# Float32 products replaced by products of parts in the last pooling group, and four steps moved around them

## The chip, the cores and the metric

The kernel runs on one core of one Trainium2 chip, in float32 throughout: inputs, outputs and sums. The metric is the time of one execution on the device in microseconds, the median of several runs. The core's engines are TensorE (matmuls; PE in the profile, and PEld for its weight loads), VectorE (DVE), ScalarE (ACT), GpSimd (POOL) and SyncE (SP), which here only issues transfers.

## What is computed

Two decoder layers on 256 tokens of 2048 features: the first mixes tokens by causal pooling over windows of 2, 4, 8 and 16 tokens, the second by latent attention. Each layer has a SwiGLU feed-forward of width 5632. The change is all in the first layer, from the pooling to the start of its feed-forward:

```python
POOL_WINDOWS = (2, 4, 8, 16)
def multiscale_pool_mixer(h, pool_w, pool_scale):
    cs = jnp.cumsum(hf, axis=1)
    for g, w in enumerate(POOL_WINDOWS):
        sl = slice(g * POOL_GROUP, (g + 1) * POOL_GROUP)      # 512 features
        c_prev = jnp.pad(cs[..., sl], ((0, 0), (w, 0), (0, 0)))[:, :S]
        count = jnp.minimum(t + 1, w)
        diff = (cs[..., sl] - c_prev) / count - hf[..., sl]
        outs.append(jnp.einsum('bsc,cd->bsd', diff, pool_w[g]))   # 512 x 512
    return jnp.concatenate(outs, axis=-1) * pool_scale
...
x = x + multiscale_pool_mixer(rms_norm(x, pool_norm[l]), pool_w[l], pool_scale[l])
x = x + swiglu(rms_norm(x, ffn_norm[l]), w_gate[l], w_up[l], w_down[l])
```

## The kernel before, in words

**Parts.** A float32 matmul is slow on TensorE, so nearly all products are made of parts. ScalarE rounds a number to the type float32r (the high part), VectorE subtracts (the low part), and TensorE adds high x high, high x low and low x high. For weights this is `split`: a chunk of 128 x 1024 lands in one of eight slots of `raw`, ScalarE writes `w_hi` (L850), VectorE writes `w_lo` (L1238), both with four slots, and signals `lo_ready`. For activations it is `gained`: ScalarE multiplies x by the norm's gain into the left half of `xg` (L862), VectorE writes the low part into the right half (L1248). `product3` (L435, L436) then takes one loaded tile of weights against 512 columns (both halves of `xg`), and its low part against 256.

**Pooling.** The pooling is linear over tokens and the product linear over features, so the kernel first multiplies and then mixes. `pool_product(g, half)` (L505) is a plain float32 matmul: `x_pool` (x times gain, made by ScalarE's `pool_gain`) is the loaded tile of 128 x 128, a chunk of pooling weights is the moving one with 512 columns. A group has four feature tiles and two halves of the tokens, so eight matmuls, four for each `half`. `product_hi` on ScalarE (L887) and `product_lo` on VectorE (L1294) scale the result by the token's norm factor `tok_rstd` and leave the parts in `z`. `mix(g)` multiplies `z` by a band matrix over tokens: four outputs of five matmuls each (L527 to L533), of which L530 takes the low part of the band's first 16 columns. `pool_out` (L1300, VectorE) adds an output to x and signals `evacuated`.

**Norm sums.** The feed-forward's norm needs the sum of squares of the new x over all 2048 features. ScalarE squares each of the 16 tiles (`group_squares`, L898) into four buffers, the halves of `cross` and `sums`; GpSimd adds them into `square_sum` (L1737). Its add of tile 10 waits for `lo_ready` to be 4. `sum_over_partitions` (L487) is a TensorE matmul with ones, in the middle of the feed-forward's third pair of chunks. ScalarE's `root_of` (L856) and VectorE's `rstd_of` (L1242) follow, in order ahead of the first `ffn_tile`: `cross` (L928), `sums` (L1318, L1322), and then `split` of chunk up0 + 7.

**Order.** Every engine runs its own list in program order and waits on semaphores. TensorE's list is: products of groups 0 to 2, with `token_squares` (L513) amid the last; mix(0); first half of group 3; mix(1); second half; mix(2); chunk up0 of the feed-forward; mix(3); chunks up0 + 1, + 2, + 3 (`first_tiles`: two tiles at once); then tiles of two chunks each. A chunk is eight times `product3`. VectorE goes group by group: four `pool_out`, four `gained`, `split` of chunk up0 + g, `product_lo(g + 2)` for g < 2. ScalarE does the same with four squares behind each `split`. After group 3 both split chunks up0 + 4 to up0 + 6. Chunks 6 and 7 of `raw` are the pooling weights of group 3.

Of the kernel before, what the change touches and what calls it, by code (L numbers as in the profile page):

```python
# [38 lines left out]
F32 = mybir.dt.float32  # L39
F32R = mybir.dt.float32r  # L40
I32 = mybir.dt.int32
ALU = mybir.AluOpType
ACT = mybir.ActivationFunctionType

P = 128
# [79 lines left out]
def chunk_elems(n):  # L125

    for ph in ("down0", "down1", "down2", "down3"):
        if CHUNK[ph] <= n < CHUNK[ph] + 2 * (LAST_DT if ph == "down3" else DT):
            return DTILES * P
    if CHUNK["heads"] <= n < CHUNK["wo"] and (n - CHUNK["heads"]) % 4 == 0:  # L130
        return TILES * P // 2
    return TILES * P


def made(n):
# [9 lines left out]
def trunk(nc, xT, positions, consts, bands, gains, pool_first, pool_w, w_kv_a, w_k_pe, w_q_a, w_kv_k, w_kv_v, w_q_nope, w_q_pe,  # L145
          w_o, w_gate, w_up, w_down, w_last, final_gain, out):
    with ExitStack() as ctx:
# [124 lines left out]
        squares_ready = sem("squares_ready")  # L272
        quarter_ready = sem("quarter_ready")
        pool_gained = sem("pool_gained")
        square_made = sem("square_made")
        ones_ready = sem("ones_ready")
        init_ready = sem("init_ready")
# [153 lines left out]
        def _(pe):  # L431
# [60 lines left out]
            for _ in range(WARM_UP):  # L492
                pe.matmul(ps[:, SCORES, 0:P], ones[:, :], ones[:, :], start=True, stop=True)  # L493

            def pool_product(g, half):

                c = 2 * g + half
                for j in range(2):
                    kt = 2 * half + j
                    pe.wait_ge(w_part[c] if c < 2 and j == 0 else landed[c], 16)  # L500
                    pe.wait_ge(pool_gained, GT * g + kt + 1)
                    for s in range(2):
                        if kt == 0 and g == 3:
                            pe.wait_ge(z_ready, 2 * (g - 2) + s + 1)
                        mm = pe.matmul(ps[:, product_bank(g, s), :], x_pool[:, GT * g + kt, s * P:(s + 1) * P],  # L505
                                       raw[:, c, j * GT * P:(j + 1) * GT * P], start=(kt == 0), stop=(kt == GT - 1))
                mm.then_inc(chunks_used, 1)
# [9 lines left out]
            def mix(g):  # L517

                pe.wait_ge(z_ready, 2 * g + 2)
                for j in range(GT):  # L520
                    t = GT * g + j
                    if t >= 4 and t not in (12, 13):
                        pe.wait_ge(evacuated, t - 3)
                    bank = mix_bank(t)
                    first_hi, first_lo = (z[:, g % 2, 0, part, j * P:(j + 1) * P] for part in range(2))
                    second_hi, second_lo = (z[:, g % 2, 1, part, j * P:(j + 1) * P] for part in range(2))
                    pe.matmul(ps[:, bank, 0:SEQ], first_hi, band[:, g, B_FIRST:B_FIRST + SEQ], start=True, stop=False)  # L527
                    pe.matmul(ps[:, bank, 0:SPILL], first_lo, band[:, g, B_FIRST:B_FIRST + SPILL], start=False,
                              stop=False)
                    pe.matmul(ps[:, bank, 0:PAD], first_hi, band[:, g, B_LOW:B_LOW + PAD], start=False, stop=False)  # L530
                    pe.matmul(ps[:, bank, P:SEQ], second_hi, band[:, g, B_SECOND:B_SECOND + P], start=False,
                              stop=False)
                    pe.matmul(ps[:, bank, P:SEQ], second_lo, band[:, g, B_SECOND:B_SECOND + P], start=False,  # L533
                              stop=True).then_inc(mixed, 1)
# [16 lines left out]
            def ffn(layer, half, xg_before, stats):  # L551
                p = 2 * layer + half
                n0, t0 = CHUNK[UPS[p]], TILE[UPS[p]]
                peel = 0
                if half == 0:
                    peel = 1
                    if layer == 0:
                        first_tiles(n0, t0, xg_before, (0,))
                        mix(GROUPS - 1)
                        first_tiles(n0, t0, xg_before, (1, 2, 3))  # L560
                    else:
                        first_tiles(n0, t0, xg_before)
                    long_tile(n0 + 4, t0 + 2, xg, TILES,
                              each=lambda kt: sum_over_partitions(stats) if kt == TILES else None)
                    long_tile(n0 + 6, t0 + 3, xg, TILES)
                with pe.Fori(0, FH // 2 - peel) as i:
                    for f in range(4):
                        long_tile(n0 + BODY * peel + 2 * f, t0 + 4 * peel + f, xg, TILES, i, 4)
                n0, t0 = CHUNK[DOWNS[p]], TILE[DOWNS[p]]
                if p == 3:  # L570
                    return

                long_tile(n0, t0, act, DTILES, each=lambda kt: pe.wait_ge(act_ready, p * FH + kt + 1))
                for d in range(1, 4):
                    long_tile(n0 + 2 * d, t0 + d, act, DTILES)
                with pe.Fori(0, DT // 4 - 1) as i:
                    for d in range(4):
                        long_tile(n0 + BODY + 2 * d, t0 + 4 + d, act, DTILES, i, 4)
# [259 lines left out]
        def _(sc):  # L838
# [51 lines left out]
            def group_gained(g):  # L890
                for t in range(GT * g, GT * g + GT):
                    gained(t, TILE["pool"] + t + 1, G_FFN0, xg)

            def group_squares(g):
                for t in range(GT * g, GT * g + GT):
                    if t >= 4:
                        sc.wait_ge(squares_added, t - 3)
                    nc.scalar.activation(square_of(t), x[:, t, :], ACT.Square).then_inc(square_made, 1)  # L898

            sc.wait_ge(gain_landed, 16)  # L900
            pool_gain(0)
# [3 lines left out]
            quarter_square(2)  # L905
            pool_gain(2)
            quarter_square(3)
            pool_gain(3)
            sc.wait_ge(stats_summed, 1)
            nc.scalar.activation(tok_root[:, :, :], ps[:, 0:2, 0:1], ACT.Sqrt, bias=eps[:, :],  # L910
                                 scale=1.0 / D_MODEL).then_inc(root_ready, 1)
            sc.wait_ge(rstd_ready, 1)
            product_hi(0)
            product_hi(1)
            for g in range(GROUPS):
                group_gained(g)
                split(CHUNK["up0"] + g)
                group_squares(g)
                if g < 2:
                    product_hi(g + 2)  # L920

            def ffn_tile(p, f, splits, i=None):

# [13 lines left out]
            def ffn(layer, half, stats):  # L937
                p = 2 * layer + half
                n0 = CHUNK[UPS[p]]
                for w in range(3):  # L940
                    split(n0 + w + SPLIT_SLOTS)
                if stats is not None:
                    root_of(stats, D_MODEL)

                def tile(f, i=None):

                    n = n0 + 4 * f + 3 + SPLIT_SLOTS
                    ffn_tile(p, f, (lambda: split(n, i), lambda: split(n + 1, i),
                                    lambda: (split(n + 2, i), split(n + 3, i))), i)

                with sc.Fori(0, FH // 2 - 1) as i:
                    tile(0, i)
                    tile(1, i)
                tile(FH - 2)

                nothing = lambda: None
                ffn_tile(p, FH - 1, (nothing, nothing, lambda: split(n0 + 4 * FH - 1 + SPLIT_SLOTS)))

                n1, t1 = CHUNK[DOWNS[p]], TILE[DOWNS[p]]
                if p == 3:  # L960
                    return

                def down(d, i=None):
                    split(n1 + 2 * d + SPLIT_SLOTS, i)
                    if half == 1 and layer == 0:
                        gained(d, t1 + d + 1, G_ATTN, xg, i, 4)
                    split(n1 + 2 * d + 1 + SPLIT_SLOTS, i)

                with sc.Fori(0, DT // 4 - 1) as i:
                    for d in range(4):  # L970
                        down(d, i)
                for d in range(DT - 4, DT):
                    down(d)
# [229 lines left out]
        def _(ve):  # L1203
# [71 lines left out]
            for q in range(4):  # L1275
                ve.wait_ge(squares_ready, q + 1)
                a, b, c = x_square[:, 4 * q:4 * q + 2, :], x_square[:, 4 * q + 2:4 * q + 4, :], x_square[:, 4 * q, :]
                step(nc.vector.tensor_tensor(a, a, b, ALU.add))
                ins = nc.vector.tensor_tensor(c, c, x_square[:, 4 * q + 1, :], ALU.add)
                if q >= 1:  # L1280
                    step(ins)
                    ins = nc.vector.tensor_tensor(c, c, x_square[:, 4 * q - 4, :], ALU.add)
                ins.then_inc(quarter_ready, 1)
                ve.wait_ge(quarter_ready, q + 1)
            ve.wait_ge(gain_landed, 16)
            ve.wait_ge(root_ready, 1)
            nc.vector.reciprocal(tok_rstd[:, :, :], tok_root[:, :, :]).then_inc(rstd_ready, 1)
            ve.wait_ge(rstd_ready, 1)
# [13 lines left out]

            product_lo(0)
            product_lo(1)
            for g in range(GROUPS):
                for t in range(GT * g, GT * g + GT):
                    pool_out(t)
# [555 lines left out]
```

## Time and profile before

| | |
|---|---|
| median of 3 runs | 1771.49 us (1771.15 to 1771.55) |
| the profiled execution | 1770.85 us, of it the span of the trace 1769.1 us |
| granted TensorE clock | 0.999 |
| TensorE busy | 1761.5 us |
| VectorE / ScalarE / GpSimd busy | 1130.7 / 914.3 / 113.1 us |
| bytes moved | 328.79 MB, 186 GB/s on average |

A row of the timeline has the start in us from the span's start, the time it took, the engine, the line, the operation, what it writes and reads, and how many like it are merged. In brackets stands how long the engine was idle ahead of it and what released it. The ends of matmuls are modelled, so TensorE's pace is read from one start to the next, best from its weight loads.

### The profile page before, as it was taken

The page shows a single profiled execution, that of the slowest core. Times are in us where ns is not written, and L with a number is a line of the kernel's source. Part 1 is how long each engine was busy: PE and PEld are TensorE (multiplying, and loading weights), DVE is VectorE, ACT ScalarE, POOL GpSimd, SP SyncE. Part 2 cuts the span into 40 slices and gives each one's busy share as a digit, 9 for nine tenths or more (in the row PEclk, how much of TensorE's full clock was granted, in tenths as well). Part 3 has the DMA queues.
Part 4 walks back from the last instruction along what each step waited for, and adds up shares of the span by engine and source line. Part 5 has one row for each costly group of instructions (what it writes and reads, how often), then busy time and mean ns, then how long its engine had stood idle before and what let it go on. Part 6 is the DMA issues. An engine that isn't in the chain of part 4 may idle for free.

```text
span 1769.1 us, 29325 instructions
## 1 busy us (share of the span) xinstructions
PE 1761.5 (100%) x10438; PEld 1564.0 (88%) x10438; DVE 1130.7 (64%) x1460; ACT 914.3 (52%) x1176; POOL 113.1 (6%) x132
## 2 busy tenths in 40 slices
PE   9999999999999999999999999999999999999998
PEld 6888888888888888889999888888888888888887
DVE  5766666556666666678997776666655566666554
ACT  6666664334444453456775466666533344445433
POOL 2100000000000001124111420000000000000000
PEclk9999999999999999999999999999999999999999
DMA  7555556545555566545445555555665455556642
GB/s 282 195 188 190 189 197 229 191 155 177 190 190 190 190 223 196 175 152 160 148 137 179 190 184 191 189 188 188 230 200 166 162 190 190 190 190 222 227 146 72
DMA packets 86017, 328.79 MB, mean 186 GB/s; under 512 B 9680, under 2 KB 11088, under 8 KB 85840
## 3 DMA queue, kind: packets, MB, share of 16 engines
q1 hardware_dynamic: 85680, 327.03, 55.5%
q10 hardware_dynamic: 288, 1.11, 0.2%
q8 instruction: 30, 0.49, 0.1%
q14 instruction: 19, 0.16, 0.0%
HBM read 326.01 MB, written 2.10 MB: 185 GB/s over the span
## 4 chain that ended last, share of the span: by engine, by line
PE 100%; DVE 0%; issue 0%; DVEq 0%; ACT 0%; POOL 0%; POOLq 0%
PE ps L435 58%; PE ps L436 31%; PE ps L505 2%; PE ps L443 1%; PE ps L445 1%; PE ps L444 1%; PE ps L799 1%; PE ps L798 1%; PE ps L797 1%; PE ps L633 0%; PE ps L632 0%; PE ps L631 0%; PE ps L685 0%; PE ps L493 0%; PE ps L705 0%; PE ps L706 0%
## 5 line engine op out<-in xcount | busy, mean ns | idle before, releaser
L1238 DVE TENSOR_TENSOR w_lo<-raw,w_hi 128x1024 fp32r<-128x1024 f32 (+2 forms) x564 | 736.0, 1308 | 419.1 <-ACT w_hi L850 416.9
L435 PE MATMUL ps<-xg,w_hi 128*128 128x512 f32 x2880 | 999.7, 390 | 0.0
L850 ACT ACTIVATE w_hi<-raw 128x1024 fp32r<-128x1024 f32 (+2 forms) x565 | 630.9, 1120 | 548.9 <-PE ps L436 533.2
L436 PE MATMUL ps<-xg,w_lo 128*128 128x256 f32 x2880 | 812.1, 282 | 0.0
L435 PEld LDWEIGHTS ps<-xg,w_hi 128*128 128x128 f32 x2880 | 540.5, 188 | 113.5 <-DVE w_lo L1238 0.3
L436 PEld LDWEIGHTS ps<-xg,w_lo 128*128 128x128 f32 x2880 | 544.3, 189 | 0.1
L435 PE MATMUL ps<-act,w_hi 128*128 128x512 f32 x1320 | 458.0, 390 | 0.0
L436 PE MATMUL ps<-act,w_lo 128*128 128x256 f32 x1320 | 372.2, 282 | 0.0
L435 PEld LDWEIGHTS ps<-act,w_hi 128*128 128x128 f32 x1320 | 247.7, 188 | 51.9
L436 PEld LDWEIGHTS ps<-act,w_lo 128*128 128x128 f32 x1320 | 249.5, 189 | 0.0
L1318 DVE TENSOR_TENSOR sums<-ps,cross 128x512 f32<-128x512 f32 x88 | 60.8, 691 | 93.1 <-ACT cross L928 93.1
L928 ACT ACTIVATE cross<-ps 128x512 f32<-128x512 f32 x88 | 52.5, 597 | 117.4 <-PE ps L436 117.0
L435 PE MATMUL ps<-heads,w_hi 128*128 128x512 f32 x256 | 89.1, 391 | 0.0
L1691 POOL TENSOR_TENSOR square<-x 128x256 f32 (+1 forms) x32 | 33.2, 1038 | 762.6 <-DVE x L1339 762.6
L436 PE MATMUL ps<-heads,w_lo 128*128 128x256 f32 x256 | 72.2, 282 | 0.0
L1338 DVE TENSOR_TENSOR x<-ps,x 128x256 f32 (+1 forms) x76 | 32.1, 422 | 54.6 <-PE ps L436 54.6
L1322 DVE TENSOR_TENSOR sums<-sums,rstd 128x512 f32<-128x512 f32 x88 | 60.9, 692 | 3.0
L931 ACT ACTIVATE gate_act<-sums 128x256 f32<-128x256 f32 x88 | 36.8, 419 | 47.3 <-DVE sums L1322 47.1
L862 ACT ACTIVATE xg<-x,gain 128x256 fp32r<-128x256 f32 (+1 forms) x48 | 23.5, 508 | 66.9 <-DVE x L1339 62.1
L435 PEld LDWEIGHTS ps<-heads,w_hi 128*128 128x128 f32 x256 | 48.0, 188 | 9.9
L436 PEld LDWEIGHTS ps<-heads,w_lo 128*128 128x128 f32 x256 | 48.4, 189 | 0.0
L443 PE MATMUL ps<-latent,w_hi 128*128 128x256 f32 x160 | 44.9, 281 | 0.0
(200 smaller groups left out, 1240.2 us busy)
## 6 DMA issues: line engine op xcount, KB each, us to landing
raw<-w_gate SPq DMA_DIRECT2D x176, 512.0 KB, 3.2
raw<-w_up SPq DMA_DIRECT2D x176, 512.0 KB, 3.2
raw<-w_down SPq DMA_DIRECT2D x120, 704.0 KB, 4.2
raw<-w_o SPq DMA_DIRECT2D x32, 512.0 KB, 3.2
raw<-w_last SPq DMA_DIRECT2D x11, 512.0 KB, 3.2
raw<-w_q_a SPq DMA_DIRECT2D x8, 512.0 KB, 3.2
raw<-w_kv_a SPq DMA_DIRECT2D x8, 512.0 KB, 3.3
raw<-w_q_nope SPq DMA_DIRECT2D x8, 512.0 KB, 3.2
```

What stands on the lines that cost most here:

```text
L435: pe.matmul(ps[:, bank, :], w_hi[:, s, j * P:(j + 1) * P], moving, start=start, stop=False)
L436: return pe.matmul(ps[:, bank, 0:SEQ], w_lo[:, s, j * P:(j + 1) * P], moving[:, 0:SEQ], start=False, stop=stop)
L443: pe.matmul(dst, w_hi[:, s, j * P:(j + 1) * P], moving[:, 0:SEQ], start=start, stop=False)
L505: mm = pe.matmul(ps[:, product_bank(g, s), :], x_pool[:, GT * g + kt, s * P:(s + 1) * P], raw[:, c, j * GT * P:(j + 1) * GT * P], start=(k ...
L850: nc.scalar.activation(dst, src, ACT.Copy).then_inc(hi_ready, 1)
L928: nc.scalar.activation(cross[:, :, :], ps[:, bank:bank + 2, SEQ:], ACT.Copy).then_inc(cross_ready, 1)
L931: nc.scalar.activation(gate_act[:, :], sums[:, 0, :], ACT.Silu).then_inc(gate_ready, 1)
L1238: nc.vector.tensor_tensor(lo, src, hi.bitcast(F32), ALU.subtract).then_inc(lo_ready, 1)
L1318: nc.vector.tensor_tensor(sums[:, :, :], ps[:, bank:bank + 2, 0:SEQ], cross[:, :, :], ALU.add).then_inc(evacuated, 2)
L1322: nc.vector.tensor_tensor(sums[:, :, :], sums[:, :, :], r, ALU.mult).then_inc(sums_ready, 1)
L1338: step(nc.vector.tensor_tensor(xd, ps[:, b, 0:SEQ], xd, ALU.add))
L1691: step(nc.gpsimd.tensor_tensor(square[:, :], src, src, ALU.mult))
```

## The change

Four things are done. Group 3 of the pooling is multiplied in parts: ScalarE writes the high part of x times gain for its four tiles into `xg` and the high part of chunks 6 and 7 into `w_hi`, VectorE writes the low parts, and `split_product` takes three matmuls of 512 columns in place of one float32 matmul. For group 0 (a window of 2, whose factors 1 and 1/2 have no low part) L530 is left out. ScalarE's squares of group 3 are no longer made in one piece: the splits of up0 + 4, + 5 and + 6 stand between them. And `sum_over_partitions` stands four `product3` later in its chunk.

```diff
+def band_is_exact(g):
+    return all(w & (w - 1) == 0 for w in range(1, WINDOWS[g] + 1))
...
+            def split_product(half):
+                c = 2 * (GROUPS - 1) + half
+                w = c % SPLIT_SLOTS
+                pe.wait_ge(pool_w_lo, half + 1)
+                for j in range(2):
+                    kt = 2 * half + j
+                    pe.wait_ge(pool_x_lo, kt + 1)
+                    wh, wl = (part[:, w, j * GT * P:(j + 1) * GT * P] for part in (w_hi, w_lo))
+                    for s in range(2):
+                        if kt == 0:
+                            pe.wait_ge(z_ready, 2 * (GROUPS - 3) + s + 1)
...
+                        pe.matmul(dst, hi, wh, start=(kt == 0), stop=False)
+                        pe.matmul(dst, hi, wl, start=False, stop=False)
+                        mm = pe.matmul(dst, lo, wh, start=False, stop=(kt == GT - 1))
+                mm.then_inc(chunks_used, 1)
...
-                    pe.matmul(ps[:, bank, 0:PAD], first_hi, band[:, g, B_LOW:B_LOW + PAD], start=False, stop=False)
+                    if not band_is_exact(g):
+                        pe.matmul(ps[:, bank, 0:PAD], first_hi, band[:, g, B_LOW:B_LOW + PAD], start=False, stop=False)
...
-                              each=lambda kt: sum_over_partitions(stats) if kt == TILES else None)
+                              each=lambda kt: sum_over_partitions(stats) if kt == TILES + 4 else None)
...
+            def pool_x_split():
+                sc.wait_ge(x_landed[GROUPS - 1], 16)
+                for t in range(DT - GT, DT):
+                    nc.scalar.activation(xg[:, t, 0:SEQ], x[:, t, :], ACT.Identity,
+                                         scale=gain[:, G_POOL + t, :]).then_inc(pool_x_hi, 1)
+
+            def pool_w_split(half):
+                c = 2 * (GROUPS - 1) + half
+                sc.wait_ge(landed[c], 16)
+                nc.scalar.activation(w_hi[:, c % SPLIT_SLOTS, 0:TILES * P], raw[:, c, 0:TILES * P],
+                                     ACT.Copy).then_inc(pool_w_hi, 1)
...
             quarter_square(3)
-            pool_gain(3)
+            pool_x_split()
+            pool_w_split(0)
             sc.wait_ge(stats_summed, 1)
...
             product_hi(1)
+            pool_w_split(1)
...
                 group_gained(g)
+                if g >= 2:
+                    sc.wait_ge(chunks_used, 2 * (GROUPS - 1) + g - 1)
                 split(CHUNK["up0"] + g)
-                group_squares(g)
+                if g < GROUPS - 1:
+                    group_squares(g)
...
-                for w in range(3):
-                    split(n0 + w + SPLIT_SLOTS)
+                if p > 0:
+                    for w in range(3):
+                        split(n0 + w + SPLIT_SLOTS)
...
             ve.wait_ge(gain_landed, 16)
+            for t in range(DT - GT, DT):
+                ve.wait_ge(pool_x_hi, t - DT + GT + 1)
+                nc.vector.scalar_tensor_tensor(
+                    xg[:, t, SEQ:], x[:, t, :], gain[:, G_POOL + t, :], xg[:, t, 0:SEQ].bitcast(F32), ALU.mult,
+                    ALU.subtract).then_inc(pool_x_lo, 1)
+            pool_w_split(0)
             ve.wait_ge(root_ready, 1)
...
             product_lo(1)
+            pool_w_split(1)
```

ScalarE's last squares and the splits of up0 + 3 to up0 + 6, from group 3's `gained` to the root of the norm. Before:

```order
L862 ACTIVATE xg<-x,gain 128x256 x4
L850 ACTIVATE w_hi<-raw 128x1024
L898 ACTIVATE cross<-x 128x256 x2
L898 ACTIVATE sums<-x 128x256 x2
L850 ACTIVATE w_hi<-raw 128x1024 x3
L856 ACTIVATE root<-ps,eps 128x256
```

And with the change (L892, L880, L927 and L886 are the same four lines of code):

```order
L892 ACTIVATE xg<-x,gain 128x256 x4
L880 ACTIVATE w_hi<-raw 128x1024
L927 ACTIVATE cross<-x 128x256 x2
L880 ACTIVATE w_hi<-raw 128x1024
L927 ACTIVATE sums<-x 128x256
L880 ACTIVATE w_hi<-raw 128x1024
L927 ACTIVATE sums<-x 128x256
L880 ACTIVATE w_hi<-raw 128x1024
L886 ACTIVATE root<-ps,eps 128x256
```

The three splits moved ahead of the second, third and fourth of the last squares' places, so that the last square stands behind two more splits than before.

VectorE, from its last sum of squares for `tok_rstd` to the split of chunk up0. Before:

```order
L1282 TENSOR_TENSOR x_square<-x_square 128x256
L1287 RECIPROCAL tok_rstd<-tok_root 128x2
L1294 SCALAR_TENSOR_TENSOR z<-ps,tok_rstd,z 128x512 x4
L1300 SCALAR_TENSOR_TENSOR x<-ps,gain,x 128x256 x4
L1248 SCALAR_TENSOR_TENSOR xg<-x,gain,xg 128x256 x4
L1238 TENSOR_TENSOR w_lo<-raw,w_hi 128x1024
```

With the change (L1353 and L1347 are new, `pool_w_split` is L1347):

```order
L1340 TENSOR_TENSOR x_square<-x_square 128x256
L1353 SCALAR_TENSOR_TENSOR xg<-x,gain,xg 128x256 x4
L1347 TENSOR_TENSOR w_lo<-raw,w_hi 128x1024
L1358 RECIPROCAL tok_rstd<-tok_root 128x2
L1365 SCALAR_TENSOR_TENSOR z<-ps,tok_rstd,z 128x512 x4
L1347 TENSOR_TENSOR w_lo<-raw,w_hi 128x1024
L1371 SCALAR_TENSOR_TENSOR x<-ps,gain,x 128x256 x4
L1306 SCALAR_TENSOR_TENSOR xg<-x,gain,xg 128x256 x4
L1296 TENSOR_TENSOR w_lo<-raw,w_hi 128x1024
```

Five instructions came in ahead of the reciprocal and one ahead of the first `pool_out`; the rest keeps its order.

## Rows read from the trace of the kernel before

**Rows 1.** The page, part 1: busy us (share of the span), instructions.
```profile
PE 1761.5 (100%) x10438; PEld 1564.0 (88%) x10438; DVE 1130.7 (64%) x1460; ACT 914.3 (52%) x1176; POOL 113.1 (6%) x132
```

**Rows 2.** Timeline, weight loads of L528 before and behind four float32 products.
```profile
27.71 0.19 PEld L528 LDWEIGHTS ps<-band,z 128*128 128x128 f32 x1
...
31.71 0.19 PEld L528 LDWEIGHTS ps<-band,z 128*128 128x128 f32 x1 [0.24 <-issue]
```

**Rows 3.** Timeline at the kernel's end: first of 24 512-column matmuls, and the next.
```profile
1751.22 0.39 PE L797 MATMUL ps<-w_hi,act 128*128 128x512 f32 x1
...
1756.81 0.28 PE L797 MATMUL ps<-w_hi,act 128*128 128x256 f32 x1
```

**Rows 4.** Timeline, weight loads of the 16-column matmul in two neighbouring outputs.
```profile
26.70 0.19 PEld L530 LDWEIGHTS ps<-band,z 128*128 128x128 f32 x1
...
27.27 0.19 PEld L530 LDWEIGHTS ps<-band,z 128*128 128x128 f32 x1
```

**Rows 5.** Timeline before mix(0), and the landing of chunks 5 to 7.
```profile
8.62 1.41 SPq L344 DMA_DIRECT2D raw<-pool_w  x3
...
DMA to landing us min/median/max: 10.7/11.5/12.3
...
22.68 0.26 ACT L910 ACTIVATE tok_root<-ps,eps 128x2 f32<-128x2 f32 x1 [4.61 <-PE ps L513]
...
23.07 0.17 DVE L1287 RECIPROCAL tok_rstd<-tok_root 128x2 f32<-128x2 f32 x1 [4.88 <-ACT tok_root L910]
...
25.60 0.19 PEld L527 LDWEIGHTS ps<-band,z 128*128 128x128 f32 x1 [0.25 <-issue]
```

**Rows 6.** Timeline of VectorE, groups 0 to 3.
```profile
26.73 2.18 DVE L1300 SCALAR_TENSOR_TENSOR x<-ps,gain,x 128x256 f32<-128x256 f32 x4
...
30.43 1.22 DVE L1238 TENSOR_TENSOR w_lo<-raw,w_hi 128x1024 fp32r<-128x1024 f32 x1
...
33.56 1.65 DVE L1300 SCALAR_TENSOR_TENSOR x<-ps,gain,x 128x256 f32<-128x256 f32 x4
...
38.56 1.41 DVE L1294 SCALAR_TENSOR_TENSOR z<-ps,tok_rstd,z 128x512 fp32r<-128x512 f32 x2 [0.58 <-ACT z L887]
...
47.45 1.23 DVE L1238 TENSOR_TENSOR w_lo<-raw,w_hi 128x1024 fp32r<-128x1024 f32 x1
```

**Rows 7.** Timeline of weight loads: mix(3), chunk up0 + 1, chunk up0 + 4.
```profile
42.33 0.19 PEld L527 LDWEIGHTS ps<-band,z 128*128 128x128 f32 x1
...
44.59 0.19 PEld L435 LDWEIGHTS ps<-xg,w_hi 128*128 128x128 f32 x1
...
53.13 0.19 PEld L435 LDWEIGHTS ps<-xg,w_hi 128*128 128x128 f32 x1 [0.26 <-DVE w_lo L1238]
```

**Rows 8.** Timeline of group 3's squares, adds and splits.
```profile
47.32 0.71 ACT L898 ACTIVATE cross<-x 128x256 f32<-128x256 f32 x2
...
48.80 1.56 POOL L1737 TENSOR_TENSOR square_sum<-square_sum,sums 128x256 f32<-128x256 f32 x2 [3.07 <-ACT cross L898]
...
50.72 2.94 ACT L850 ACTIVATE w_hi<-raw 128x1024 fp32r<-128x1024 f32 x3
...
51.80 1.28 DVE L1238 TENSOR_TENSOR w_lo<-raw,w_hi 128x1024 fp32r<-128x1024 f32 x1 [3.12 <-ACT w_hi L850]
...
52.08 1.60 POOL L1737 TENSOR_TENSOR square_sum<-square_sum,sums 128x256 f32<-128x256 f32 x1
...
53.00 1.76 DVE L1238 TENSOR_TENSOR w_lo<-raw,w_hi 128x1024 fp32r<-128x1024 f32 x1
...
53.76 1.60 POOL L1737 TENSOR_TENSOR square_sum<-square_sum,sums 128x256 f32<-128x256 f32 x1
```

**Rows 9.** Timeline from the sums' matmul to chunk up0 + 7.
```profile
55.91 0.31 PEld L487 LDWEIGHTS ps<-square_sum,ones 128*128 128x128 f32 x2
...
60.55 1.22 DVE L1238 TENSOR_TENSOR w_lo<-raw,w_hi 128x1024 fp32r<-128x1024 f32 x1
...
61.91 0.19 PEld L435 LDWEIGHTS ps<-xg,w_hi 128*128 128x128 f32 x1
```

More of the change, by code:

```diff
@@ L274, in trunk @@
         pool_gained = sem("pool_gained")
+        pool_x_hi = sem("pool_x_hi")
+        pool_x_lo = sem("pool_x_lo")
+        pool_w_hi = sem("pool_w_hi")
+        pool_w_lo = sem("pool_w_lo")
         square_made = sem("square_made")
@@ L493, in _ @@
                 pe.matmul(ps[:, SCORES, 0:P], ones[:, :], ones[:, :], start=True, stop=True)
+            def split_product(half):
[9 more added lines that the diff above has]
+                            pe.wait_ge(z_ready, 2 * (GROUPS - 3) + s + 1)
+                        dst = ps[:, product_bank(GROUPS - 1, s), :]
+                        hi, lo = (xg[:, DT - GT + kt, part * SEQ + s * P:part * SEQ + (s + 1) * P] for part in range(2))
+                        pe.matmul(dst, hi, wh, start=(kt == 0), stop=False)
+                        pe.matmul(dst, hi, wl, start=False, stop=False)
+                        mm = pe.matmul(dst, lo, wh, start=False, stop=(kt == GT - 1))
+                mm.then_inc(chunks_used, 1)
             def pool_product(g, half):
                 c = 2 * g + half
+                if g == GROUPS - 1:
+                    split_product(half)
+                    return
                 for j in range(2):
@@ L502, in pool_product @@
                     for s in range(2):
-                        if kt == 0 and g == 3:
-                            pe.wait_ge(z_ready, 2 * (g - 2) + s + 1)
                         mm = pe.matmul(ps[:, product_bank(g, s), :], x_pool[:, GT * g + kt, s * P:(s + 1) * P],
@@ L892, in group_gained, with tile_square @@
                     gained(t, TILE["pool"] + t + 1, G_FFN0, xg)
+            def tile_square(t):
+                if t >= 4:
+                    sc.wait_ge(squares_added, t - 3)
+                nc.scalar.activation(square_of(t), x[:, t, :], ACT.Square).then_inc(square_made, 1)
             def group_squares(g):
                 for t in range(GT * g, GT * g + GT):
-                    if t >= 4:
-                        sc.wait_ge(squares_added, t - 3)
-                    nc.scalar.activation(square_of(t), x[:, t, :], ACT.Square).then_inc(square_made, 1)
+                    tile_square(t)
+            def pool_x_split():
[8 more added lines that the diff above has]
+                                     ACT.Copy).then_inc(pool_w_hi, 1)
             sc.wait_ge(gain_landed, 16)
@@ L914, in _ @@
             product_hi(1)
+            pool_w_split(1)
             for g in range(GROUPS):
                 group_gained(g)
+                if g >= 2:
+                    sc.wait_ge(chunks_used, 2 * (GROUPS - 1) + g - 1)
                 split(CHUNK["up0"] + g)
-                group_squares(g)
+                if g < GROUPS - 1:
+                    group_squares(g)
                 if g < 2:
                     product_hi(g + 2)
+            tile_square(DT - 4)
+            tile_square(DT - 3)
+            split(CHUNK["up0"] + SPLIT_SLOTS)
+            tile_square(DT - 2)
+            split(CHUNK["up0"] + 1 + SPLIT_SLOTS)
+            tile_square(DT - 1)
+            split(CHUNK["up0"] + 2 + SPLIT_SLOTS)
             def ffn_tile(p, f, splits, i=None):
@@ L1284, in _, with pool_w_split @@
                 ve.wait_ge(quarter_ready, q + 1)
-            ve.wait_ge(gain_landed, 16)
+            def pool_w_split(half):
+                c = 2 * (GROUPS - 1) + half
+                w = c % SPLIT_SLOTS
+                ve.wait_ge(pool_w_hi, half + 1)
+                nc.vector.tensor_tensor(w_lo[:, w, 0:TILES * P], raw[:, c, 0:TILES * P],
+                                        w_hi[:, w, 0:TILES * P].bitcast(F32), ALU.subtract).then_inc(pool_w_lo, 1)
+            ve.wait_ge(gain_landed, 16)
+            for t in range(DT - GT, DT):
[4 more added lines that the diff above has]
+            pool_w_split(0)
             ve.wait_ge(root_ready, 1)
```

## The prediction

> **What bounds the kernel now.** The page first: TensorE is busy for 1761.5 us of a span of 1769.1 us [rows 1], and the chain that ended last is TensorE for 100% of the span. So only what makes TensorE start a piece earlier or later counts. The change touches the first 62 us alone; from there on the loops are the same. I therefore read the timeline of those 62 us and ask one thing: when does TensorE start the weight chunk after which nothing waits any more? I number the first feed-forward's chunks c0 to c7 (`up0` + 0 to 7). c0 to c3 are `first_tiles`, c4 and c5 are the tile that carries `sum_over_partitions`, c6 and c7 the next. The load for c7 starts at 61.91 [rows 9]. The final time moves by as much as this start does.
>
> **Products of parts.** Pool group 3 has 8 float32 products (4 feature tiles, 2 token halves). Between one weight load of `mix` (that of L528) in its last output and the same in the next mix lie four such products and one output: 27.71 to 31.71 is 4.00 us [rows 2], less 0.57 for an output (26.70 to the same load of the next output at 27.27, five loads [rows 4]). That leaves 3.43 us for four, 6.87 us for eight. The new form has 24 matmuls of 512 columns. The end of the kernel runs exactly such a row of 24: from 1751.22 to 1756.81, 5.59 us [rows 3]. TensorE saves 6.87 - 5.59 = 1.28 us, 0.64 us in each half. Bounds: nothing, if changing between kinds of product cost as much, and 1.9 us at 0.21 us for a matmul, a quarter of a float32 product's 0.858.
>
> **The zero low band.** Four matmuls of 16 columns go in group 0. They are short, yet every matmul of `mix` is paced by its weight load, 0.11 us apart [rows 4]. Four go: 0.45 us (bounds 0 and 0.45, since the pace is that regular). Together, TensorE would be 1.73 us earlier at the last `mix`, if nothing else ended last. The rest of the sum is what ends last instead.
>
> **Before the first mix.** ScalarE now splits half a weight chunk pair (chunk 6) before the square root, and VectorE takes four low parts of x and the chunk's low part before its reciprocal. Chunk 6 is the second of three loads issued from 8.62; they took 10.7, 11.5 and 12.3 us, so it lands near 9.09 + 11.5 = 20.6 [rows 5]. ScalarE ends its split at 21.65, before the 22.68 of its square root. VectorE starts its part 1.08 behind ScalarE's start, as at 50.72 and 51.80 [rows 8], so at 21.7, and ends at 22.9; its reciprocal stood at 23.07 [rows 5]. So it costs nothing, with 0.1 us to spare. If the chunk landed 1 us later, it would cost nearly 1 us. Below nothing it can't go, since the root waits for TensorE.
>
> **VectorE's second low part.** `pool_w_split(1)` stands in VectorE between the scaled products and `pool_out(0)`, 1.22 us by the like split at 30.43 [rows 6]. Queued behind it are all of group 0's outputs, ScalarE's `gained`, and so every later step of both engines. Some comes back: the first four `pool_out` took 2.18 us because TensorE's mix paced them, and take 1.65 us, as at 33.56, when all is there [rows 6]. The shift is 1.22 - 0.53 = 0.69 us. After that VectorE is busy from 38.56 to 48.68 without a gap, so the shift stays (bounds: 0, if gaps near 32 took it, and 1.22). ScalarE's part costs nothing: it stood waiting for the first `pool_out` there.
>
> **What is late next.** The last `mix` waits for the low parts of group 3, ready at 38.56 + 1.41 = 39.97 and now at 40.66. TensorE's own count brings it there at 42.33 - 1.73 = 40.60 [rows 6, 7]. With 0.11 us from a VectorE end to a weight load (the split of 51.80, 1.22 us of work, let TensorE go at 53.13 [rows 7, 8]) it waits about 0.15 us. c1 then starts at 44.59 - 1.58 = 43.01 [rows 7], and c3 could start two chunks of 2.78 us later, at 48.57. But c3 needs VectorE's fourth split, which ended at 47.45 + 1.23 = 48.68 and now ends at 49.37 [rows 6]: c3 starts at 49.48, a wait of 0.9 us. The 0.2 us wait before c4 goes, since ScalarE's split for it no longer follows the last squares. c4 starts at 52.26, c5 at 55.04, which was 55.91: of 1.73 us, 0.87 us are left.
>
> **The sums.** They move from c5's first to its fifth product, 4 x 0.347 = 1.39 us later, so TensorE would reach them at 56.43. What hangs on them is serial: ScalarE's root, VectorE's reciprocal, then the first tile's `cross`, its two VectorE steps, and only then VectorE's split for c7. From the sums' load at 55.91 to that split's end at 60.55 + 1.22 = 61.77 are 5.86 us [rows 9]. TensorE arrived at c7 at 61.91, so this chain had 0.1 us to spare before. Moving the sums 1.39 us towards c7 must make TensorE wait. c7 now starts 5.86 + 0.11 = 5.97 us behind the sums, whatever was saved ahead.
>
> **Can the sums be ready?** GpSimd's last six adds wait for the fourth split. Before the change they began at 48.80, four ran 0.82 us apart with VectorE idle, and only the last two met VectorE's splits [rows 8]. Now ScalarE splits between the squares: squares at 48.01, the first split at 48.63 (both from 47.32 [rows 8] plus the shift), VectorE's part at 49.70, while GpSimd's add of 49.49 runs. The rows show what a meeting costs. VectorE's split of 53.00 took 1.76 us and ended 1.08 us after GpSimd's add (52.08 + 1.60 = 53.68); the next add ended 0.60 us after that split (55.36 after 54.76). All three splits and the adds beside them take turns now: 50.23, 51.31, 51.91, 52.99, 53.59, 54.67, 55.27. Two adds alone follow, at 0.82 us: the last ends at 56.91. It is later than TensorE's 56.43, so TensorE waits at the sums until 57.0, and c7 starts at 57.0 + 5.97 = 62.97. Against 61.91 that is **1.06 us later**.
>
> The Trainium skill ("SBUF — State Buffer", Who interferes with whom) says that a VectorE instruction with two SBUF inputs and a GpSimd instruction that reads SBUF exclude each other, and that the second blocks until the first is done. The trace agrees on the taking of turns, with 1.76 us for a split that alone takes 1.22. Taken strictly it gives the third rival's sum; the rows show less than a full repeat.
>
> **The rivals.** (1) GpSimd isn't late, because the adds slip in between the splits: six at 0.82 us end at 54.4, TensorE's own 56.43 decides, c7 starts at 62.40, 0.5 us later than before. For it: two of the splits leave gaps. Against: the 1.76 us. (2) The saving survives: VectorE's shift is swallowed, c3 doesn't wait, and the adds are done in time. Sums at 55.91 - 1.73 - 0.21 + 1.39 = 55.36, c7 at 61.33, 0.6 us earlier. Against it: VectorE has no gap from 38.56 on. (3) The engine that loses a turn does its whole work after the winner: 0.74 for an add, 1.23 for a split. The six adds end at 57.78, c7 starts at 63.8, 1.9 us later. Against: 1.08 and 0.60 in the rows. (4) Slower by more: chunk 6 lands late. ScalarE's split stands in order ahead of the square root, so from a landing at 20.7 on each us of delay is one us at the first `mix` and at everything behind. The neighbouring load landed at 21.9, which would be about 1.2 us more, 2.3 in all; over 0.2% (3.5 us) needs a landing after 23.1. The matmuls not being saved at all is no rival with a time of its own: c7 hangs on the sums, and they on GpSimd, so up to 1 us of TensorE's saving could be missing with little change.
>
> **How the numbers follow.** The forecast has 0.45, rival 1 0.22, rival 2 0.14, rival 3 0.12, rival 4 0.07 (of it 0.02 beyond 3.5 us). The profiled execution took 1770.85 us for a span of 1769.1, and would take 1771.9 for a span of 1770.2. The median of the runs is 1771.49, 0.64 us above the profiled one, so the forecast is 1771.49 + 1.06 = 1772.5 us. The range goes from rival 2 (1770.9) to rival 3 (1773.4), with 0.3 us at either end for the spread of the runs: 1770.6 to 1773.7. A measurement of this kernel can tell about 0.2% from no change, 3.5 us. No saving of TensorE is that large, so faster gets 0.01, slower 0.02, the rest is no change.
>
> **What would show it.** In the changed trace: eight products in about 5.6 us; first mix at 25.6; a TensorE wait of about 0.9 us before c3 on VectorE's split; GpSimd adds of 1.4 to 1.6 us from 49.5 on; TensorE waiting at the sums on GpSimd; a wait of 1.3 us or more before c7 on VectorE's split; c7 at 63.0. The forecast is wrong if c7 needs no wait, or if ScalarE's square root starts after 22.7.

## The result, and the profile after

The changed kernel takes 1773.47 us (median of 22 runs, 1772.83 to 1773.84), the kernel before beside it 1771.3 us (22 runs, 1770.85 to 1772.25). The ratio is 1.0012, 95% interval 1.0006 to 1.0017: 2.2 us slower, clear of the scatter of the runs but inside the 0.2% that the prediction calls no change. The profiled execution took 1773.69 us, its span is 1771.9 us.

The page of the changed kernel has one group that waits where the kernel before had none (`product3` on VectorE's low part; columns: busy us, mean ns | idle before, releaser):

```profile
PE 1761.6 (99%) x10442; PEld 1565.4 (88%) x10442; DVE 1134.8 (64%) x1466; ACT 916.3 (52%) x1178; POOL 114.4 (6%) x132
...
L444 PE MATMUL ps<-xg,w_hi 128*128 128x512 f32 x2880 | 1000.0, 390 | 2.6 <-DVE w_lo L1296 2.6
```

TensorE is as busy as before [rows 1] (1761.6 against 1761.5 us) in a longer span: the work that it was spared doesn't show in this sum, perhaps because its first products ran slower in this execution (last section; in e9, where they didn't, it was busy for 1760.5 us). In the timeline of its weight loads every place of the prediction can be seen: first mix, last mix, chunk up0 + 3, the sums, chunk up0 + 7, and a sixth, chunk + 7 of the second layer:

```profile
26.53 0.19 PEld L556 LDWEIGHTS ps<-band,z 128*128 128x128 f32 x1 [0.24 <-issue]
...
41.54 0.19 PEld L556 LDWEIGHTS ps<-band,z 128*128 128x128 f32 x1
...
50.17 0.19 PEld L444 LDWEIGHTS ps<-xg,w_hi 128*128 128x128 f32 x1 [0.86 <-DVE w_lo L1296]
...
57.71 0.30 PEld L496 LDWEIGHTS ps<-square_sum,ones 128*128 128x128 f32 x2 [0.66 <-POOL square_sum L1809]
...
63.61 0.19 PEld L444 LDWEIGHTS ps<-xg,w_hi 128*128 128x128 f32 x1 [1.35 <-DVE w_lo L1296]
...
1048.65 0.19 PEld L444 LDWEIGHTS ps<-xg,w_hi 128*128 128x128 f32 x1 [1.33 <-DVE w_lo L1296]
```

From the first mix to the last it takes TensorE 15.01 us, before the change 16.73 (25.60 [rows 5] to 42.33 [rows 7]): 1.72 us are saved. From the first mix to chunk + 7 it takes 37.08 us, before 36.31 [rows 5, 9]: all is gone and 0.77 us more. The second layer adds a wait of 1.33 us. The sum is 2.10 us, the difference of the medians 2.17. The two spans differ by 2.8 us: the profiled executions reach the first mix 0.93 us apart (last section), and behind chunk + 7 of the second layer the changed one takes 0.2 us less, whose cause isn't shown.

VectorE and GpSimd from the fourth split on (first VectorE, then GpSimd):

```profile
48.90 1.22 DVE L1296 TENSOR_TENSOR w_lo<-raw,w_hi 128x1024 fp32r<-128x1024 f32 x1
50.46 1.62 DVE L1296 TENSOR_TENSOR w_lo<-raw,w_hi 128x1024 fp32r<-128x1024 f32 x1 [0.34 <-ACT w_hi L880]
52.43 1.32 DVE L1296 TENSOR_TENSOR w_lo<-raw,w_hi 128x1024 fp32r<-128x1024 f32 x1 [0.35 <-ACT w_hi L880]
54.10 1.33 DVE L1296 TENSOR_TENSOR w_lo<-raw,w_hi 128x1024 fp32r<-128x1024 f32 x1 [0.35 <-ACT w_hi L880]
...
50.25 2.42 POOL L1809 TENSOR_TENSOR square_sum<-square_sum,sums 128x256 f32<-128x256 f32 x2 [3.06 <-ACT cross L927]
52.75 3.29 POOL L1809 TENSOR_TENSOR square_sum<-square_sum,cross 128x256 f32<-128x256 f32 x2
56.12 1.55 POOL L1809 TENSOR_TENSOR square_sum<-square_sum,sums 128x256 f32<-128x256 f32 x2
```

Six adds take from 50.25 to 57.67, and TensorE takes up the sums at 57.71. Before, the six took from 48.80 to 55.36 [rows 8]. Counted from the first mix they end at 31.14 us, before at 29.76: 1.38 us later, 0.5 us because they begin later (as VectorE's fourth split does) and 0.86 us because they take longer (7.42 against 6.56).

### The profile page after: what moved, and what is told of

Read it like the earlier page. It is cut to its first block, busy times and chain, and to the rows that moved or that the text cites. A ratio compares the mean times of both kernels' runs of the same rounds, so it can differ in the third digit from the quotient of the medians.

```text
span 1771.9 us, 29341 instructions
## 1 busy us (share of the span) xinstructions
PE 1761.6 (99%) x10442; PEld 1565.4 (88%) x10442; DVE 1134.8 (64%) x1466; ACT 916.3 (52%) x1178; POOL 114.4 (6%) x132
## 4 chain that ended last, share of the span: by engine, by line
PE 97%; DVE 1%; ACT 1%; POOL 0%; issue 0%; DMA 0%; DVEq 0%; SPq 0%; POOLq 0%; ACTq 0%
PE ps L444 57%; PE ps L445 30%; PE ps L452 1%; PE ps L453 1%; PE ps L454 1%; PE ps L534 1%; PE ps L829 1%; PE ps L828 1%; PE ps L827 1%; PE ps L663 0%; PE ps L662 0%; PE ps L661 0%; POOL square_sum L1809 0%; DVE z L1365 0%; PE ps L715 0%
## 5 line engine op out<-in xcount | busy, mean ns | idle before, releaser
L880 ACT ACTIVATE w_hi<-raw 128x1024 fp32r<-128x1024 f32 (+2 forms) x565 | 631.1, 1120 | 548.5 <-PE ps L445 532.6
L892 ACT ACTIVATE xg<-x,gain 128x256 fp32r<-128x256 f32 (+1 forms) x48 | 23.2, 507 | 66.9 <-DVE x L1411 62.1
```

The costliest lines, as they stand in the source:

```text
L880: nc.scalar.activation(dst, src, ACT.Copy).then_inc(hi_ready, 1)
L892: nc.scalar.activation(dst[:, plus(t, i, per), 0:SEQ], x[:, plus(t, i, per), :], ACT.Identity, scale=gain[:, plus(col + t, i, per), :]).th ...
```

## The experiments

Each kernel was timed in 11 runs beside the kernel before, whose medians were 1771.33 us (e1 to e4), 1771.59 (e5 to e8) and 1771.41 (e9 to e11). "Norm" is the time from TensorE's first mix to chunk + 7 of the first layer (layer 0), which leaves out how late the first mix was: 36.31 us before, 37.08 us with the change. The intervals of the ratios reach 0.0009 to either side, 1.6 us. So the medians alone settle only that e1, e4 to e7 and e11 are slower than the kernel before; all finer differences rest on the traces. The changed kernel's norm came out alike twice (37.08 and 37.11), and the norm's loss plus the wait in layer 1 gives the difference of the medians to about 0.3 us in every run but e8.

**e1: the kernel before, only the sums later.**

```diff
-   each=lambda kt: sum_over_partitions(stats) if kt == TILES else None)
+   each=lambda kt: sum_over_partitions(stats) if kt == TILES + 4 else None)
```

> The kernel before with one edit: the sums stand four products later, in both layers. Theory S (a serial chain of 5.97 us from the sums to chunk up0 + 7 of each layer sets TensorE back by what the sums moved): a TensorE wait of 1.3 us before chunk + 7 in layer 0 and another in layer 1, +2.6 us in all against before. Rival P (the loss of the changed kernel comes from the pooling stage, VectorE's extra low part and the start of the products): no wait, within 0.3 us of before. Rival H (the sums were late for GpSimd's adds anyway): +1.3 us, from layer 1 alone.

Measured: 1773.93 us, 2.60 us more than before (ratio 1.0015, 1.0006 to 1.0024). Weight loads of its sums and of chunk + 7, in layer 0 and in layer 1:

```profile
57.37 0.31 PEld L487 LDWEIGHTS ps<-square_sum,ones 128*128 128x128 f32 x2
...
63.28 0.19 PEld L435 LDWEIGHTS ps<-xg,w_hi 128*128 128x128 f32 x1 [1.34 <-DVE w_lo L1238]
...
1042.40 0.31 PEld L487 LDWEIGHTS ps<-square_sum,ones 128*128 128x128 f32 x2
...
1048.30 0.19 PEld L435 LDWEIGHTS ps<-xg,w_hi 128*128 128x128 f32 x1 [1.33 <-DVE w_lo L1238]
```

Chunk + 7 starts 5.91 and 5.90 us behind the sums. One edit of the four, alone, costs more than the whole change, 1.3 us in each layer. Rivals P and H fall. In layer 0 of the changed kernel the sums wait for GpSimd besides, so this price can't be carried over to it (see the account below).

**e2: the changed kernel, layer 1's sums where they were.**

```diff
-   each=lambda kt: sum_over_partitions(stats) if kt == TILES + 4 else None)
+   each=lambda kt: sum_over_partitions(stats) if kt == (TILES if layer else TILES + 4) else None)
```

> The changed kernel, but the sums of layer 1 stand where they stood before; layer 0 keeps them four products later. Theory S: the wait of 1.33 us before layer 1's chunk + 7 goes and nothing takes its place, -1.3 us against the changed kernel, +0.8 us against before. Rival P: no change against the changed kernel, +2.2 us against before.

Measured: 1771.98 us, 0.65 us more than before (ratio 1.0003, 0.9994 to 1.0012), 1.5 us less than the changed kernel's difference. The trace settles it: no wait is left in layer 1, layer 0 is unchanged (norm 37.11). Theory S holds for layer 1.

**e3: chunk + 7 split before the root.** In `ffn` of ScalarE and VectorE the first pair of tiles is taken out of the loop for half 0, and its first split goes ahead:

```diff
-                    for w in range(3):
+                    for w in range(3 + (half == 0)):
                         split(n0 + w + SPLIT_SLOTS)
...
+                peel = 1 - half
+                if peel:
+                    tile(0, ahead=True)
+                    tile(1)
```

> The changed kernel, but in both layers chunk + 7 is split before the root of the norm, on ScalarE and VectorE, so it no longer hangs on the sums. Theory S: both waits before chunk + 7 go (1.35 and 1.33 us); chunk + 8 is next, whose split ends about 7.4 us behind the sums where TensorE comes 7.3 us behind them, so 0.1 to 0.3 us of wait appears there. -2.3 us against the changed kernel, about -0.1 us against before. Rival: the next split is as late and takes the whole wait over, no change against the changed kernel.

Measured: 1771.58 us, 0.25 us more than before (ratio 1.0001, 0.9992 to 1.001). No wait before chunk + 7 or + 8 in either layer. But in layer 0 the fourth split of VectorE meets GpSimd's adds as well, and the sums come later:

```profile
58.24 0.30 PEld L496 LDWEIGHTS ps<-square_sum,ones 128*128 128x128 f32 x2 [1.49 <-POOL square_sum L1818]
```

That is 1.49 us of wait where the changed kernel has 0.66. The theory holds, but for this new cost. The edit did one thing more: an ACT_TABLE_LOAD of 1.28 us that stood on ScalarE between the root and the first `cross` is gone, 38 of 40 such loads of the two lines in the whole kernel (ScalarE is busy for 869.5 us, not 916.3). VectorE's first step behind `cross` starts 3.09 us behind the sums, not 3.30, which may be why the 0.1 to 0.3 us of wait expected at chunk + 8 didn't come. The same holds for e8 to e10, which have the same edit of the loop.

**e4: the low band kept.** `if not band_is_exact(g):` becomes `if True:`.

> The changed kernel, but group 0's four 16-column matmuls on the low band are kept. If chunk + 7 hangs on the sums and these on GpSimd's adds, TensorE's 0.45 us is covered by its waits at chunk + 3 and at the sums: the time of the changed kernel within 0.2 us. Rival (TensorE's own count sets the end): +0.45 us against the changed kernel.

Measured: 1773.17 us, 1.84 us more than before (ratio 1.0011, 1.0002 to 1.002). The norm is 37.09, that of the changed kernel 37.08. The 0.44 us show in TensorE's wait before chunk + 3, 0.42 us where the changed kernel has 0.86:

```profile
50.03 0.19 PEld L444 LDWEIGHTS ps<-xg,w_hi 128*128 128x128 f32 x1 [0.42 <-DVE w_lo L1296]
```

So the matmuls left out save what was forecast, and it is worth nothing there.

**e5: the splits behind the squares.** The three `split` calls stand behind `tile_square(DT - 1)` again. (In the changed kernel one stands ahead of the third square, one ahead of the fourth and the last behind it.)

> The changed kernel, but ScalarE's splits of chunks up0 + 4 to up0 + 6 stand behind the four last squares again. GpSimd's adds then run 0.82 us apart until VectorE's splits begin and end earlier, but VectorE's split for chunk + 4 ends 1.6 us later. Theory (TensorE then waits before chunk + 4 on VectorE, 1.5 us, and not at the sums): the sums come 1.0 us later than in the changed kernel and so does the end, +1.0 us against it. Rival L (the taking of turns between VectorE and GpSimd is the dear part): the sums come earlier, -0.6 us.

Measured: 1774.48 us, 2.89 us more than before (ratio 1.0016, 1.0007 to 1.0025). The norm is 38.14, 1.06 us more than the changed kernel's. The wait moved to chunk + 4; the sums don't wait:

```profile
54.66 0.19 PEld L444 LDWEIGHTS ps<-xg,w_hi 128*128 128x128 f32 x1 [1.68 <-DVE w_lo L1296]
...
58.82 0.31 PEld L496 LDWEIGHTS ps<-square_sum,ones 128*128 128x128 f32 x2
```

Splitting amid the squares is worth 1.1 us in the trace (0.7 us in the medians), although it makes the adds 0.9 us slower. Rival L falls.

**e6: VectorE's second low part later.**

```diff
             product_lo(1)
-            pool_w_split(1)
...
                 split(CHUNK["up0"] + g)
+                if g == 0:
+                    pool_w_split(1)
```

> The changed kernel, but VectorE makes the low part of the second chunk of pooling weights behind the split of chunk up0, not ahead of the first outputs. Theory (VectorE's later steps are late by this instruction, and the sums hang on them through GpSimd's adds): VectorE's fourth split comes 0.5 us earlier, the wait before chunk + 3 falls from 0.86 to about 0.4 us, -0.5 us against the changed kernel. Rival (the shift is made elsewhere or hidden): no change.

Measured: 1773.44 us, 1.85 us more than before (ratio 1.001, 1.0001 to 1.0019), norm 37.14. The expectation of 0.5 us less missed. In its new place the instruction meets GpSimd's first add and takes 1.76 us, not 1.22:

```profile
31.97 1.76 DVE L1347 TENSOR_TENSOR w_lo<-raw,w_hi 128x1024 fp32r<-128x1024 f32 x1
```

The fourth split stands 22.42 us behind the first mix, 22.37 in the changed kernel: the engine's shift is the same, made elsewhere.

**e7: float32 products, all else as changed.** `split_product`, `pool_x_split` and both `pool_w_split` are out, `pool_gain(3)` is back.

> The changed kernel with float32 products in group 3 as before and without the steps that make the parts; band, splits and sums as changed. TensorE has 1.28 us more work, VectorE 1.22 us less ahead of its first output. Theory (what the parts save is all spent in waits on VectorE and GpSimd): the wait before chunk + 3 and the one at the sums go, the end stays within 0.3 us of the changed kernel. Rival (the saving of TensorE counts): +1.3 us against the changed kernel.

Measured: 1773.32 us, 1.73 us more than before (ratio 1.001, 1.0001 to 1.0019), norm 36.94 against 37.08. Neither chunk + 3 nor the sums wait; chunk + 7 does, 1.34 us. TensorE did 1.28 us more (16.29 us from the first mix to the last, not 15.01) and came to chunk + 7 0.14 us earlier; the loss in the medians is 0.4 us smaller than the changed kernel's, which the intervals don't settle. What the products of parts save is all given back. The rival falls.

```profile
57.27 0.31 PEld L496 LDWEIGHTS ps<-square_sum,ones 128*128 128x128 f32 x2
...
63.17 0.19 PEld L444 LDWEIGHTS ps<-xg,w_hi 128*128 128x128 f32 x1 [1.34 <-DVE w_lo L1293]
```

**e8: float32 products, with the chain taken off.** e7 with the splits of e3 and the sums two products later in layer 0 and as before in layer 1.

> Float32 products in group 3, group 0's zero low band left out, the splits amid the last squares, chunk + 7 split before the root in both layers, the sums two products later in layer 0 and where they were in layer 1. Theory: no wait before chunk + 3, + 4 or + 7; the sums hang on GpSimd at about the time TensorE comes; TensorE's 0.45 us and the 0.26 us wait before chunk + 4 are won: 0.5 to 0.7 us less than before. Rival: GpSimd's adds, which now meet four splits of VectorE, take it back: the time of before.

Measured: 1771.18 us, 0.41 us less than before (ratio 0.9998, 0.9989 to 1.0007). The direction isn't settled by the interval, and the trace shows no gain in the first layer: chunk + 7 starts 36.36 us behind the first mix, before 36.31. The sums wait 0.80 us for GpSimd, whose adds met four splits, as the rival said.

**e9: products of parts, with the chain taken off.** As the changed kernel, but ScalarE splits chunk + 7 ahead of its root, VectorE behind its reciprocal, and layer 1's sums stand where they were:

```diff
                 if stats is not None:
                     rstd_of(stats)
+                if half == 0:
+                    split(n0 + 3 + SPLIT_SLOTS)
```

> The changed kernel (products of parts and all), with chunk + 7 no longer behind the sums: ScalarE splits it ahead of the root, VectorE behind its reciprocal, in both layers; the sums of layer 1 where they stood before. Theory: no wait before chunk + 7; in layer 0 the sums still wait 0.6 us for GpSimd and chunk + 8 then starts about where it did before the change; layer 1 loses nothing. The time of before within 0.3 us, 2.0 us less than the changed kernel. Rival (the sums' chain only moves to chunk + 8): at least 1 us more than before.

Measured: 1771.84 us, 0.43 us more than before (ratio 1.0003, 0.9993 to 1.0012), which is between the two. Chunk + 7 doesn't wait, chunk + 8 does. The profile names no releaser, but VectorE's split for it ended 0.13 us earlier, at 65.01. Its steps for the first tile now stand behind the split of chunk + 7: the first starts 4.18 us behind the sums, in e3 3.09.

```profile
65.14 0.19 PEld L444 LDWEIGHTS ps<-xg,w_hi 128*128 128x128 f32 x1 [1.05 <-issue]
```

Part of the chain's price had only moved on. Both this kernel and the one before come to the first mix at the same time (25.57 and 25.60), so their starts of chunk + 8 can be set side by side: 65.14 here, 61.91 + 2.77 = 64.68 before, 0.46 us later, as the medians say (0.43).

**e10: as e9, with float32 products, and the sums two products later in layer 0 as in e8.**

> The kernel of float32 products, no zero low band, splits amid squares, with VectorE's split of chunk + 7 behind its reciprocal, so GpSimd's adds meet three splits and not four; sums two products later in layer 0. Theory (the 0.80 us wait at the sums was the fourth meeting, 0.87 us): that wait goes, 0.7 us less than with the split ahead, 1.1 us less than before. Rival (VectorE's later sums make chunk + 8 wait instead): as with the split ahead, 0.4 us less than before.

Measured: 1771.05 us, 0.36 us less than before (ratio 0.9999, 0.999 to 1.0008). The wait at the sums went as expected, but 0.35 us of wait at chunk + 8 came:

```profile
64.91 0.19 PEld L444 LDWEIGHTS ps<-xg,w_hi 128*128 128x128 f32 x1 [0.35 <-issue]
```

That is 38.71 us behind the first mix (26.20), before 39.08: 0.37 us earlier, as the median says (e8 has 39.13 there, though its median is as low). By the traces it gains 0.4 us on e8 where 0.7 were expected; by the medians nothing. The runs can't tell e8, e10 and before apart.

**e11: the changed kernel again.**

> The changed kernel unaltered, beside the others on this chip: 2.1 us more than before (0.8 us from layer 0 and 1.33 us from layer 1), and a second trace, for how far TensorE's arrival at the first mix differs from one execution to the next: between 25.6 and 26.6 us if that start is a matter of the execution, again near 26.5 if it belongs to the program.

Measured: 1773.55 us, 2.14 us more than before (ratio 1.0012, 1.0003 to 1.0021). First mix at 26.24, norm 37.11, waits of 0.87, 0.66, 1.35 and 1.34 us at the same four places.

## Why the prediction was right, and where it fell short

It forecast 1772.5 us in a range of 1770.6 to 1773.7, no change beyond 0.2%, and a loss of 1.06 us. Measured were 1773.47 us and a loss of 2.17 us. In layer 0 the mechanism was right; in all, the size was half, for want of layer 1. That the time still lies in the range is in part luck: the upper end was set by rival 3, which didn't occur, and the 1.33 us that filled the room came from a place the prediction had put at nothing.

**The step that failed** is a sentence of the first part, "The change touches the first 62 us alone". `sum_over_partitions` is placed in `ffn`, which runs for half 0 of both layers, and the diff's line has no condition on the layer. The 5.97 us chain, worked out for layer 0, is in layer 1 as well, with TensorE arriving just as late (before the change chunk + 7 started 5.99 us behind the sums there). It costs 1.33 us there (e1; e2 takes it away). With that term the sum would have been 2.4 us.

**Step by step** for layer 0:

- Products of parts and zero band: 1.73 us forecast, 1.72 measured between first and last mix. e7 confirms 1.28 us for the products, e4 0.45 us for the band.
- Before the first mix: no cost, as forecast. VectorE's low part ran at 21.76, its reciprocal waited for the root. In e9, which has the same instructions up to there, the reciprocal started right behind the low part at 22.95, and the first mix at 25.57 (before 23.07 and 25.60).
- A sign of being wrong that the prediction named came up: ScalarE's square root started at 23.62, after 22.7. It wasn't chunk 6 landing late. The split began at 20.67, where 20.6 was forecast, and the root stood waiting for TensorE:

```profile
20.67 1.06 ACT L942 ACTIVATE w_hi<-raw 128x1024 fp32r<-128x1024 f32 x1 [2.57 <-DMA raw<-pool_w]
...
23.62 0.26 ACT L956 ACTIVATE tok_root<-ps,eps 128x2 f32<-128x2 f32 x1 [1.89 <-PE ps L542]
```

  The prediction took the start of the first mix for a fixed number; it differs by up to 1 us between executions (last section), so this sign couldn't tell its rival 4.
- VectorE's shift: 0.69 us forecast. The fourth split stands 22.37 us behind the first mix, before it was 21.85 [rows 5, 6], so 0.52. Mis-sized was the instruction put in: the first `pool_out` started 1.02 us later relative to the mix, not 1.22. The split holds up the next instruction by 1.13 us (27.55 to 28.68), and all of VectorE's steps from the reciprocal on came 0.09 us earlier relative to the mix.
- The last mix: 0.15 us of wait forecast, none measured; it follows from the smaller shift. Before chunk + 3: 0.9 forecast, 0.86 measured.
- GpSimd's adds: forecast to end 7.54 us behind the end of the fourth split, measured 7.55 (50.12 to 57.67). The taking of turns, read from the meetings in the trace before, held for three splits. Rival 1, without turns, and rival 3, with whole repeats (8.4 us), are both out. At the sums TensorE waited 0.66 us; about 0.6 was forecast.
- Chunk + 7: 5.97 us behind the sums forecast, 5.90 measured. The 0.11 us in it, from a VectorE end to a weight load, were misread: the split of 51.80 took 1.28 us, not 1.22, and 0.05 us are left [rows 7, 8], as measured now (63.56 to 63.61). Likewise the sums start 0.04 us behind the last add, not 0.09. In all the norm was to be 37.37 and is 37.08, 0.3 us less.
- Rival 2 (the saving survives) fell: e4 and e7 give TensorE 0.45 and 1.28 us more work and change the norm by +0.01 and -0.14. Rival 4 (late landing) didn't occur.

**What wasn't tested** is the changed kernel with layer 0's sums in their old place. The prediction blames their new place for the wait before chunk + 7, and that wait is there. But GpSimd's last add ends at 57.67 wherever the sums stand, so they could start at 57.71 at the earliest. From the old place TensorE has 6.00 us of work to chunk + 7 (55.91 to 61.91 [rows 9]), which gives 63.71 as an estimate; measured is 63.61. By that estimate the new place costs nothing in layer 0 of the changed kernel, and the 0.77 us are those of the late adds. In e1 and e7, whose adds are done before TensorE comes, the new place is what costs.

So the forecast time came out 1.0 us low, mainly by two errors of opposite sign, 1.3 us left out and 0.3 us too much; the kernel before, at 1771.3 us, also came out 0.2 us below the 1771.49 that the forecast started from.

## What to carry to other kernels

Before a wait or a sum is moved towards its consumer, measure the whole serial chain behind it and the slack at its far end. Here 5.9 us of chain had 0.1 us of slack, so moving its start by 1.39 us, alone (e1), cost 1.3 us in each of the two layers. Count every place where an edited helper runs, not only the one that it was edited for. Ask also what else holds the moved step: in layer 0 of the changed kernel it was GpSimd, and there the move changed nothing by the estimate above. And work taken off TensorE pays only if the engines that feed it don't fall behind: of the 1.7 us saved nothing reached chunk + 7, since one instruction more on VectorE and a third meeting of its splits with GpSimd's adds (two before) made the adds end 1.38 us later.

## What the runs showed of the hardware that wasn't expected

**TensorE's first products.** In some executions the first float32 products run at half the usual pace. Weight loads of the changed kernel, with 0.86 us between the first two rows, where 0.43 is usual:

```profile
5.91 0.34 PEld L534 LDWEIGHTS ps<-raw,x_pool 128*128 128x128 f32 x1 [0.52 <-issue]
6.77 0.20 PEld L534 LDWEIGHTS ps<-raw,x_pool 128*128 128x128 f32 x1 [0.52 <-issue]
7.20 0.19 PEld L534 LDWEIGHTS ps<-raw,x_pool 128*128 128x128 f32 x1 [0.24 <-issue]
```

And of e9, which has the same instructions up to there:

```profile
4.77 0.30 PEld L534 LDWEIGHTS ps<-raw,x_pool 128*128 128x128 f32 x2 [0.28 <-issue]
5.31 0.19 PEld L534 LDWEIGHTS ps<-raw,x_pool 128*128 128x128 f32 x1 [0.24 <-issue]
5.74 0.19 PEld L534 LDWEIGHTS ps<-raw,x_pool 128*128 128x128 f32 x1 [0.24 <-issue]
```

The granted clock of 4.8 to 7.0 us reads 1.00 in both, the higher of its two levels. In other traces the pace is usual and the loads wait for a transfer instead (e7: 5.77, then 7.22 with 1.26 us of idle on `DMA raw<-pool_first`). The first mix came at 25.57 to 26.59 us in the thirteen traces. The instructions up to there don't settle it alone: the changed kernel had 26.53 and 26.24, e9, the same up to there, 25.57 at the usual pace. But the program isn't cleared either: the slow start stands in seven of the eight traces with products of parts and in none of the five with float32 products. The profiled execution of before (1770.85 us, first mix at 25.60) was 0.45 us below the median of its 22 runs, that of the changed kernel (26.53) 0.22 above. This is why the spans differ by 2.8 us and the medians by 2.17, and why differences between traces are better taken from the first mix on. What halves the pace isn't shown.

**VectorE and GpSimd taking turns.** A split that starts while GpSimd adds took 1.28 to 1.76 us, by how early in the add it starts, alone 1.22; an add that starts during a split took up to 1.6 us, alone 0.74. The engine that waits ends 1.08 us (split) or 0.60 us (add) after the other, some 0.14 us less than it takes alone. The Trainium skill ("SBUF — State Buffer", Who interferes with whom) calls the ports that the two share an exclusive lock; the turns agree. The 0.14 us suggest that a little of an instruction lies outside the lock, which no run tests. It isn't bound to this place: e6 moved one instruction to a free spot of VectorE and found GpSimd there.
